# Three of four squared MLP blocks turned by VectorE and copied by ScalarE, instead of turned by TensorE

## The reference

```python
        u = _rmsnorm(h, norm_mlp_g[layer])
        a = jnp.einsum('bsd,df->bsf', u, w_up[layer])
        a = jnp.square(jax.nn.relu(a))
        h = h + jnp.einsum('bsf,fd->bsd', a, w_down[layer])
```

## Time and profile before

| | before |
|---|---|
| runs | 2271.87, 2273.13, 2276.51 us |
| median | 2273.13 us |
| the profiled execution | 2273.41 us |
| its span, first to last instruction | 2271.7 us |
| mean granted clock of TensorE | 0.996 |
| busy share of the span: TensorE matmul / weight load | 99% / 81% |
| busy share: VectorE / ScalarE / GpSimd | 71% / 47% / 10% |

### The profile page before, as it was taken

One profiled execution on the slowest core, in us unless ns is written; L12 is line 12 of the kernel. 1 busy time (PEld: TensorE's weight loads), 2 busy tenths in 40 slices (PEclk: granted clock), 3 DMA queues, 4 the chain that ended last, 5 costly groups with the idle time before them and its releaser, 6 DMA issues.

```text
span 2271.7 us, 28668 instructions
## 1 busy us (share of the span) xinstructions
PE 2250.4 (99%) x10201; PEld 1850.2 (81%) x10201; DVE 1624.2 (71%) x2109; ACT 1077.6 (47%) x1307; POOL 223.6 (10%) x361
## 2 busy tenths in 40 slices
PE   9999999999999999999999999999999999999998
PEld 7888888888888888888878877787888888888886
DVE  6998789888888987997778674556555545555556
ACT  5446455445444545445563454545444344434444
POOL 0111001111111111110011000000210011100110
PEclk9999999999999999999999999999999999999999
DMA  8983678888888788887778663655666666665663
GB/s 300 325 270 121 199 247 306 304 290 293 275 293 283 263 309 286 273 270 230 234 231 258 206 207 125 207 187 170 220 195 192 215 198 210 195 195 194 200 193 126
DMA packets 249995, 527.96 MB, mean 232 GB/s; under 512 B 22144, under 2 KB 22544, under 8 KB 248592
## 3 DMA queue, kind: packets, MB, share of 16 engines
q1 hardware_dynamic: 214256, 405.32, 54.5%
q0 software_dynamic: 33664, 116.17, 14.9%
q10 hardware_dynamic: 1952, 4.85, 0.6%
HBM read 517.87 MB, written 4.21 MB: 230 GB/s over the span
## 4 chain that ended last, share of the span: by engine, by line
PE 98%; DVE 1%; ACT 1%; issue 0%; DMA 0%; SPq 0%; ACTq 0%; DVEq 0%
PE acc L1803 30%; PE acc L1812 30%; PE acc L1807 30%; PE tp L1874 2%; PE acc L1825 0%; PE acc L1830 0%; PE acc L1835 0%; PE tp L2178 0%; PE tp L2196 0%; PE tp L2190 0%; PE acc L1985 0%; PE tp L2105 0%; PE acc L1858 0%; PE acc L1856 0%; PE acc L1857 0%; PE m L1971 0%
## 5 line engine op out<-in xcount | busy, mean ns | idle before, releaser
L571 ACT ACTIVATE whi<-wring 128x1024 fp32r<-128x1024 f32 x766 | 801.7, 1051 | 1035.7 <-PE acc L1812 1034.4
L1072 DVE TENSOR_TENSOR wlo<-wring,whi 128x1024 fp32r<-128x1024 f32 x762 | 916.2, 1215 | 483.4 <-ACT whi L571 478.5
L1803 PE MATMUL acc<-whi,xhi 128*128 128x512 f32 x2056 | 557.5, 393 | 0.1
L1807 PE MATMUL acc<-whi,xlo 128*128 128x512 f32 x2056 | 549.9, 389 | 0.0
L1812 PE MATMUL acc<-wlo,xhi 128*128 128x512 f32 x2056 | 549.8, 389 | 0.0
L1803 PEld LDWEIGHTS acc<-whi,xhi 128*128 128x128 f32 x2056 | 382.4, 188 | 87.8 <-issue 9.5
L1807 PEld LDWEIGHTS acc<-whi,xlo 128*128 128x128 f32 x2056 | 386.0, 188 | 80.9
L1812 PEld LDWEIGHTS acc<-wlo,xhi 128*128 128x128 f32 x2056 | 386.0, 188 | 80.5
L1104 DVE SCALAR_TENSOR_TENSOR macc<-mring,csil,macc 128x512 f32<-128x512 f32 x480 | 344.2, 747 | 36.5 <-DMA mring<-w_mod 29.8
L466 POOL DMA_DIRECT2D mring<-w_mod x192 | 139.1, 725 | 1048.5 <-DVE macc L1104 1001.8
L1803 PE MATMUL acc<-whi,ahi 128*128 128x512 f32 x608 | 164.5, 392 | 0.0
(11 more groups left out here) (275 smaller groups left out, 1251.1 us busy)
## 6 DMA issues: line engine op xcount, KB each, us to landing
wring<-w_up SPq DMA_DIRECT2D x216, 512.0 KB, 4.7
wring<-w_down SPq DMA_DIRECT2D x216, 512.0 KB, 5.3
mring<-w_mod POOLq DMA_DIRECT2D x192, 512.0 KB, 5.2
wring<-w_in SPq DMA_DIRECT2D x184, 512.0 KB, 4.9
wring<-w_gate SPq DMA_DIRECT2D x88, 512.0 KB, 4.4
wring<-w_out SPq DMA_DIRECT2D x64, 512.0 KB, 4.9
tmpT<-blk POOLq DMA_DIRECT2D x128, 32.0 KB, 3.4
gbig<-ctx_in POOLq DMA_DIRECT2D x2, 1024.0 KB, 7.0
```

Source lines behind the costliest of these rows:

```text
L571: act.activation(whi[:, piece_slot(c, piece), 0:half], wring[:, g4, piece * half:(piece + 1) * half], ACT.Copy).then_inc(hi_done, 1)
L1072: dve.tensor_tensor(wlo[:, h4, 0:half], wring[:, g4, piece * half:(piece + 1) * half], whi[:, h4, 0:half].bitcast(F32), ALU.subtract).then ...
L1803: pe.matmul(acc[:, 2 * pair + t, :], hi[:, tile, t * P:(t + 1) * P], whi[:, h4, w], start=(tile == starts), stop=False)
L1807: pe.matmul(acc[:, 2 * pair + t, :], lo[:, tile, t * P:(t + 1) * P], whi[:, h4, w], start=False, stop=False)
```

## The change

Blocks 0, 1 and 2 of each chunk are no longer turned by TensorE; block 3 still is.

- The ReLU now writes `blk` and the square is taken in place, so that `blk2` is free; from j = 1 on ScalarE waits ahead of the ReLU until VectorE has turned the block before.
- VectorE turns the block in 32 x 32 squares into `blk2` (`turn_relu`, two operations) behind its group 4j + 1, for j = 1, 2 and 3.
- ScalarE copies the sixteen strips of 32 partitions x 256 elements to their quarters in `tmpT` (`move_relu`, four at a time): behind groups 4j + 2 and 4j + 3 of the same block, and 4j and 4j + 1 of the next.
- Directly behind that last portion, ScalarE rounds four tiles (`round_relu`) and VectorE subtracts four times (`remain_relu`). For blocks 0, 1 and 2 that is at j = 2, 3 and 4, behind group 4j + 1.
- TensorE waits ahead of the first down block (j = 4, kg = 0) for the remainders of blocks 0 and 1, and ahead of its kg = 2 for those of block 2.
- The sums of `w_mod` are turned into a place of their own, `mod_turns`.

```diff
@@ constants @@
+MLP_MOVED = 3
-X_HI = 2 * (2 * KG - 1) + 4 * KG + 8 * MLP_CHUNKS + 2 * KG + 2 * KG + 8
+X_HI = 2 * (2 * KG - 1) + 4 * KG + 2 * MLP_CHUNKS + 2 * KG + 2 * KG + 8
...
-            sb("gap", [P, D], scope=ph)
+            mod_turns = sb("mod_turns", [P, 2, 2 * NB], scope=ph)
...
@@ ScalarE @@
                 if first:
                     act.wait_ge(rstd_done, 2)
+                if j:
+                    act.wait_ge(relu_turned, c.at("rt", T, T))
+                    c.add("rt")
                 for t in range(T):
-                    last = act.activation(blk2[:, t, :], acc[:, 2 * (j % 2) + t, :], ACT.Relu, scale=rstd[:, 1, t:t + 1])
+                    last = act.activation(blk[:, t, :], acc[:, 2 * (j % 2) + t, :], ACT.Relu, scale=rstd[:, 1, t:t + 1])
...
-                act.activation(blk[:, :, :], blk2[:, :, :], ACT.Square).then_inc(blk_ready, 1)
+                act.activation(blk[:, :, :], blk[:, :, :], ACT.Square).then_inc(blk_ready, 1)
                 c.add("blk")
+
+            def move_relu(j):
+
+                if j == 0:
+                    act.wait_ge(relu_turned, c.at("rm", T, T))
+                    act.wait_ge(relu_lo, c.at("rm", 0, KG))
+                for i in range(4):
+                    moved_rows = act.activation(placed[32 * j:32 * j + 32, i, :], strips[32 * i:32 * i + 32, j, :], ACT.Copy)
+                moved_rows.then_inc(relu_moved, 1)
+
+            def round_relu(tile):
+
+                act.wait_ge(relu_moved, c.at("rm", 4, 4))
+                for k in range(KG):
+                    act.activation(xhi[:, tile + k, :].rearrange("p (t i b) -> p t i b", t=T, i=4),
+                                   moved[:, k], ACT.Copy).then_inc(relu_hi, 1)
+                c.add("rm")
...
                     round_group(4 * j)
...
+                    if 2 <= j <= 4:
+                        move_relu(2)
                     round_group(4 * j + 1)
                     if first and j == 0:
                         root(1)
-                    if 1 <= j <= 4:
-                        round_banks(xhi, 4 * (j - 1), 2)
+                    if 2 <= j <= 4:
+                        move_relu(3)
+                        round_relu(4 * (j - 2))
+                    if j == 4:
+                        round_banks(xhi, 12, 2)
                     round_group(4 * j + 2)
+                    if 1 <= j <= 3:
+                        move_relu(0)
                     round_group(4 * j + 3)
+                    if 1 <= j <= 3:
+                        move_relu(1)
                     if j < 4:
                         wait_block(2)
                         relu_square(j, first and j == 0)
...
@@ VectorE @@
-                    last = dve.transpose(tmpT[:, 1 - who, :], macc[:, who, :])
+                    last = dve.transpose(turns[:, 1 - who, 0:NB], macc[:, who, :])
...
+            def turn_relu():
+
+                dve.wait_ge(blk_ready, c.at("blk", 1))
+                dve.wait_ge(relu_moved, c.at("rt", 0, 4))
+                for t in range(T):
+                    dve.transpose(turned[:, t], blk[:, t, :].rearrange("p (k j b) -> p k j b", k=KG, j=4)).then_inc(relu_turned, 1)
+                c.add("rt")
+
+            def remain_relu(tile):
+                for k in range(KG):
+                    dve.wait_ge(relu_hi, c.at("rk", 1))
+                    dve.tensor_tensor(xlo[:, tile + k, :].rearrange("p (t i b) -> p t i b", t=T, i=4), moved[:, k],
+                                      xhi[:, tile + k, :].bitcast(F32).rearrange("p (t i b) -> p t i b", t=T, i=4),
+                                      ALU.subtract).then_inc(relu_lo, 1)
+                    c.add("rk")
...
                     if g % 4 == 1 and 1 <= j <= 4:
-                        remain_banks(xhi, xlo, 4 * (j - 1), 2)
+                        if j >= 2:
+                            remain_relu(4 * (j - 2))
+                        if j < 4:
+                            turn_relu()
+                        c.add("blk")
+                        if j == 4:
+                            remain_banks(xhi, xlo, 12, 2)
                     if g in MLP_TURNED and not (last and g == 31):
-                        if last and g > min(CTX_TURNS):
-                            dve.wait_ge(tp_free, c.at("q", 2))
-                        turn_mod(MLP_TURNED[g] == SC1)
+                        turn_mod(MLP_TURNED[g] == SC1, mod_turns)
...
@@ TensorE @@
                     for kg in range(3):
+                        if j == 4 and kg in (0, 2):
+                            pe.wait_ge(relu_lo, c.at("rs", KG * (2 if kg == 0 else 3), KG))
                         multiply(hi, lo, (kg,), 4, pair)
                         if first and j == 0 and kg == 0:
                             turn_added(3)
-                        if kg == 1 and 1 <= j <= 4:
+                        if kg == 1 and j == 4:
                             pe.wait_ge(blk_ready, c.at("blk", j))
                             turn_rows(blk, 2)
```

More of the change, by code:

```diff
@@ L258, in two_blocks @@
             sem(n) for n in ("squares_turned", "rows_moved", "moved_hi", "moved_lo"))
+        relu_turned, relu_moved, relu_hi, relu_lo = (
+            sem(n) for n in ("relu_turned", "relu_moved", "relu_hi", "relu_lo"))
         out_s = sem("out_s")
@@ L372, in two_blocks @@
         BANKS = {"z": 1, "suffix": 1, "ctx_state": 1, "state": 2, "turn": 1, "out": 1, "conv": 2}
-        T_O = 8 + 8 + 8 * MLP_CHUNKS + 8 + 8 + 4 + BANKS["out"] + sum(
+        T_O = 8 + 8 + 2 * MLP_CHUNKS + 8 + 8 + 4 + BANKS["out"] + sum(
             BANKS.get(step[0], 0) for steps in BESIDE[1].values() for step in steps)
@@ L850, in _ @@
             root_and_scale(2, u_g, u_g)
-            with c.loop(act, MLP_CHUNKS - 1, 1, g=32, q=8, half=4, blk=4, ha=4, ssq=4 * T):
+            with c.loop(act, MLP_CHUNKS - 1, 1, g=32, q=2, half=4, blk=4, ha=4, ssq=4 * T, rt=MLP_MOVED, rm=MLP_MOVED):
                 mlp_chunk()
@@ L1107, in mod_steps, with turn_mod, sum_mod @@
                     c.add("m")
-            def turn_mod(dual):
+            def turn_mod(dual, turns=tmpT):
                 dve.wait_ge(mod_acc, c.at("ma", 8))
                 for who in (1, 0) if dual else (0,):
-                    last = dve.transpose(tmpT[:, 1 - who, :], macc[:, who, :])
+                    last = dve.transpose(turns[:, 1 - who, 0:NB], macc[:, who, :])
                 last.then_inc(mod_turned, 1)
                 c.add("turns")
-            def sum_mod(kind, i, dual):
+            def sum_mod(kind, i, dual, turns=tmpT):
                 n = 2 if dual else 1
@@ L1122, in sum_mod @@
                 for who in range(n):
-                    last = dve.reduce_sum(parts[:, who, 0, :], tmpT[:, 1 - who, :].rearrange("p (b j) -> p b j", j=32), AX_X)
+                    last = dve.reduce_sum(parts[:, who, 0, :], turns[:, 1 - who, 0:NB].rearrange("p (b j) -> p b j", j=32), AX_X)
                 last.then_inc(mod_summed, 1)
@@ L1393, in mlp_chunk @@
                     if g % 4 == 1 and 1 <= j <= 4:
-                        remain_banks(xhi, xlo, 4 * (j - 1), 2)
+                        if j >= 2:
[5 more added lines that the diff above has]
+                            remain_banks(xhi, xlo, 12, 2)
                     if g in MLP_TURNED and not (last and g == 31):
-                        if last and g > min(CTX_TURNS):
-                            dve.wait_ge(tp_free, c.at("q", 2))
-                        turn_mod(MLP_TURNED[g] == SC1)
+                        turn_mod(MLP_TURNED[g] == SC1, mod_turns)
                     if g in MLP_SUMMED and not (last and g == 31):
                         kind = MLP_SUMMED[g]
-                        sum_mod(kind, i, kind == SC1)
+                        sum_mod(kind, i, kind == SC1, mod_turns)
                         if last and kind == SC1:
@@ L1421, in _ @@
             norm_scale(2, u_g, u_g)
-            with c.loop(dve, MLP_CHUNKS - 1, 1, g=32, q=8, hi=8, m=32, ma=80, sets=4, turns=4) as i:
+            with c.loop(dve, MLP_CHUNKS - 1, 1, g=32, q=2, hi=2, m=32, ma=80, sets=4, turns=4, blk=4, rt=MLP_MOVED,
+                        rk=KG * MLP_MOVED) as i:
                 mlp_chunk(i)
@@ L2069, in mlp_chunk @@
                 c.add("blk", 4)
+                c.add("rs", MLP_MOVED)
             mlp_chunk(True)
-            with c.loop(pe, MLP_CHUNKS - 1, 1, g=32, q=8, ha=4, half=4, blk=4):
+            with c.loop(pe, MLP_CHUNKS - 1, 1, g=32, q=2, ha=4, half=4, blk=4, rs=MLP_MOVED):
                 mlp_chunk()
```

## The result

| | before | changed |
|---|---|---|
| median of the runs | 2272.85 us | 2297.32 us |
| lowest to highest | 2271.87 to 2276.51 us | 2296.25 to 2300.46 us (4 runs) |
| the profiled execution / its span | 2273.41 / 2271.7 us | 2296.25 / 2294.4 us |
| mean granted clock | 0.996 | 0.992 |

The ratio is 1.0112, with a 95% interval of 1.0100 to 1.0124: slower, as forecast, but by 24.5 us where 15.3 were forecast, and 0.3 us above the range of 2278 to 2297 us.

A forecast was written before the change was run, and what follows sets the result against it. It took TensorE, busy for 99%, to bound the kernel. Four chunks x (4.6 us wait + 1.9 us clock) lose 26.0 us and the turns win 10.7: 15.3 us slower, 2288.4 us, range 2278 to 2297.

The forecast's parts named there:

- The turns, 10.7 us: MLP chunks: three block turns fewer on TensorE in each of four chunks, 12 x 0.89 = 10.7 us won.
- The new wait ahead of kg = 2: First down block: TensorE waits for block 2's last remainder, standing 4.6 us in each chunk.
- VectorE's list: VectorE's work from group 9 to the last four subtractions, without slack: E9 + 49.0, that is E17 + 5.4 us.
- E17: The moment TensorE ends its own group 17 in a chunk, reckoned 43.6 us behind its group 9.
- Which chain ends last: Behind the new wait: VectorE's chain at E17 + 5.4 us, later than ScalarE's at E17 + 3.9 us.
- The clock, 1.9 us a chunk: Behind the new wait, matmuls restart at a granted clock of 0.50, losing 1.9 us a chunk; bounds 0 and about 3.
- The first rival: The standstill comes as computed but the clock stays up: 2280.8 us, chance 0.17.
- in the MLP chunks TensorE never waits: MLP chunks: only work taken off TensorE's list or waits put on it change the time; no size of its own.
- its own range of 2284 to 2293: Range in us of the forecast case alone, wait and low clock together, which had chance 0.60.
- Late pieces as well: VectorE's backlog reaches TensorE's group 16, or low clock lasts 6 us: 2 to 3 us more a chunk, 2296 to 2300, chance 0.10.
- Faster: Busiest engine TensorE loses 2% of its work, wait short or absent: 2268.4 us, or 2262.4 with no wait; chance 0.05.

## Why the prediction was partly wrong

- **The turns, 10.7 us.** Right. Two blocks fewer give 1.82 us a chunk, 0.91 a turn.
- **The new wait ahead of kg = 2.** Right in place, number and cause: four waits for `xlo`, behind the turn of block 3. Its size was 5.05 us on average against 4.6. VectorE's list, reckoned from group 9 to end at E17 + 5.4 us, ended at 420.73 us with E17 at 414.92, E17 + 5.8. Over four chunks 1.8 us.

```profile
414.92 1.04 PE L1927 MATMUL tp<-tabs,blk 128*128 128x128 f32 x8
419.30 1.43 DVE L1424 TENSOR_TENSOR xlo<-tmpT,xhi 128x256 fp32r<-128x256 f32 x4
420.78 2.05 PE L1856 MATMUL acc<-whi,xhi 128*128 128x512 f32 x4 [4.82 <-DVE xlo L1424]
```

- **Which chain ends last.** Right: VectorE's, and cutting its steps made ScalarE's the last. ScalarE's was mis-sized. I had priced a strip at 0.31 us from start to start by the 128-partition roundings; it is 0.42 (four in 1.69 us). At group 17 this stayed hidden behind VectorE, but at group 9, where VectorE's list sets out, it did not. The second chunk, where TensorE's group 9 ends at 553.09 us (E9):

```profile
553.09 1.07 PE L1856 MATMUL acc<-whi,ahi 128*128 128x512 f32 x4
553.29 1.07 ACT L574 ACTIVATE whi<-wring 128x1024 fp32r<-128x1024 f32 x1 [1.00 <-PE acc L1865]
554.38 1.69 ACT L829 ACTIVATE tmpT<-blk 32x256 f32<-32x256 f32 x4
556.11 1.34 ACT L836 ACTIVATE xhi<-tmpT 128x256 fp32r<-128x256 f32 x4
556.56 1.49 DVE L1424 TENSOR_TENSOR xlo<-tmpT,xhi 128x256 fp32r<-128x256 f32 x4 [0.94 <-ACT xhi L836]
...
600.92 1.43 DVE L1424 TENSOR_TENSOR xlo<-tmpT,xhi 128x256 fp32r<-128x256 f32 x4
```

  VectorE starts at E9 + 3.5 us where 2.7 were reckoned, 0.8 us late, having waited for ScalarE. From there to its end at 602.35 us its list takes 45.8 us without a wait, 0.5 us less than the 46.3 that were reckoned. So two errors of opposite sign are behind the small miss, and the dearer strips are a good part of the one that lengthened the wait.

- **The clock, 1.9 us a chunk.** Right in kind, and filling the wait gave it back. It was 2.2 us on average, 1.3 us over four chunks. The sum also counts 0.1 us a chunk twice, since the matmuls behind a turn lose that much in any case. The first rival, a clock that holds, is out, and I had given it too much: behind none of the waits of 3.9 us or more, in any kernel, did it hold.
- **What was missing, and put the time outside the range.** No term of the sum, and no rival, was for the stop at the loop's top, 6.0 us. The step that failed is "in the MLP chunks TensorE never waits, and time is won by whatever is taken off its list and lost by any wait that is put on it": it took for granted that taking instructions out leaves the flow of the others untouched. The change made TensorE's loop lie otherwise, and at the jump back it stood 1.2 and 2.8 us in a wait that no engine ended, and then ran at the low clock. The three misses, 6.0, 1.8 and 1.3 us, are 9.1 us together, and account for the 8.9 us between 2288.4 and 2297.3. Without this one the changed kernel takes 2290.7 us, 2.3 us above the forecast and inside its own range of 2284 to 2293.
- **Late pieces as well.** The measured time lies in this rival's 2296 to 2300 us, but by luck. No piece was late, as reckoned, and of its other half, a low clock of 6 us, there was one case in four (from 602.4 to about 608.5 us, a loss of 3.0 us). *Faster* did not come; that TensorE was the most occupied engine said nothing of a wait put on it. The same 12 turns do pay, 7 us, once the last of them is not asked for too early and the loop lies well.

## What to carry to other kernels

Work taken off the engine that is always busy pays only if its last result is ready when it is asked for: put a hand-over from slower engines a whole group ahead of its use, and add up the list of the engine that writes last over every step since it last had slack. A standstill costs its own length and then the slow matmuls behind it, here 5 and 2 us. When a timeline shows an engine idle for "issue" at the top of a loop, compare the instruction queue's packets between kernels and move the loop by a few instructions ahead of it before judging the change itself.

## What the runs showed of the hardware that was not expected

- TensorE stood 3.7 to 6.4 us at the jump back to a loop's top in five of the thirteen profiles, and not at all in the others, with 83 against 74 instruction packets. Eight short matmuls ahead of the loop took it away; four inside each chunk didn't. What in the place decides (a border of what is loaded at once, or the distance of the jump) was not tried. That the packets are TensorE's own is read from their going together with its stop; the page doesn't name an engine for them.
- A copy of 32 partitions x 256 elements on ScalarE took 0.415 us, and four took 1.69 us, while four of 128 partitions x 256 took 1.33 us. The fewer partitions were no cheaper, and the copies hardly overlapped. Whether that comes from the partitions or from copying between quarters was not told apart.
- Where the matmuls came back from an equal wait, the loss was 1.75 us in two chunks and 2.4 and 3.0 us in the others of one execution: a restart has no fixed price. Over all the waits of 3.9 us or more, in any kernel, it was 1.5 to 3.0 us.
